# The convolution stage of a hybrid mixer: gate rows, fourth tap and norms moved among its blocks

## What is computed

```python
def causal_dwconv_silu(x, w):                 # CONV_K = 4 taps, each channel by itself
    y = lax.conv_general_dilated(x, w.astype(x.dtype)[:, None, :], ..., padding=[(CONV_K - 1, 0)], feature_group_count=x.shape[-1])
    return jax.nn.silu(y)

def hybrid_mixer(h, w_in, conv_w, a_log, dt_bias, ...):
    proj = h @ w_in
    qkv_a, z_a, b_a, a_a, qkv_b, f_b, gates = split_cols(proj, IN_SIZES)
    qkv_a = causal_dwconv_silu(pad_front(qkv_a), conv_w)          # 3072 channels
    qa, ka, va = split_cols(qkv_a, (A_QK, A_QK, A_V))
    qa = l2_norm(qa.reshape(B_, Lp, H_A, DK_A)) * (DK_A ** -0.5)  # 8 heads of 128
    ka = l2_norm(ka.reshape(B_, Lp, H_A, DK_A))
    beta = pad_front(jax.nn.sigmoid(b_a))                         # 8 columns
    g = pad_front(-jnp.exp(a_log) * jax.nn.softplus(a_a + dt_bias))
    o_a = gated_delta_rule(qa, ka, va, beta, g)[:, PAD:]
    ...
    log_f = jax.nn.log_sigmoid((f_b + f_bias).astype(jnp.float32))
    o_b = forgetting_attention(pad_front(qb), pad_front(kb), pad_front(vb), pad_front(log_f))[:, PAD:]
    ...
```

## Time and profile before

| | |
|---|---|
| median of 3 runs | 2016.93 us (2012.76 to 2021.17) |
| the profiled execution | 2013.64 us, of which 2012.3 us are the span of the profile |
| TensorE busy | 1793.0 us, 89% of the span |
| VectorE, ScalarE, GpSimd busy | 1237.6, 705.1, 434.5 us |
| mean granted clock of TensorE | 0.933 |

### The profile page before, as it was taken

One profiled execution on the slowest core, in us unless ns is written; L12 is line 12 of the kernel. 1 busy time (PEld: TensorE's weight loads), 2 busy tenths in 40 slices (PEclk: granted clock), 3 DMA queues, 4 the chain that ended last, 5 costly groups with the idle time before them and its releaser, 6 DMA issues. The chain is left out here.

```text
span 2012.3 us, 23773 instructions
## 1 busy us (share of the span) xinstructions
PE 1793.0 (89%) x9472; PEld 1356.0 (67%) x9472; DVE 1237.6 (62%) x2172; ACT 705.1 (35%) x1201; POOL 434.5 (22%) x373
## 2 busy tenths in 40 slices
PE   7989999999999989799989999977887878787878
PEld 6869988877899869678979778874333333333333
DVE  4766645765566448545464455767777667666754
ACT  4545534344455344533342343422212121212211
POOL 0330000400000000003022000014554544454541
PEclk9989999999999979889999998988998988889889
DMA  6324554444455533312221212567999999999996
GB/s 263 118 92 168 189 188 168 168 168 167 152 191 186 189 121 126 126 37 83 92 86 62 84 64 84 202 269 291 421 421 422 422 421 422 421 421 422 421 422 249
DMA packets 62621, 453.57 MB, mean 225 GB/s; under 512 B 6944, under 2 KB 7072, under 8 KB 7856
## 3 DMA queue, kind: packets, MB, share of 16 engines
q0 software_dynamic: 36864, 268.45, 32.1%
q1 hardware_dynamic: 25040, 178.27, 24.6%
q10 hardware_dynamic: 608, 5.34, 0.7%
HBM read 450.98 MB, written 1.05 MB: 225 GB/s over the span
## 5 line engine op out<-in xcount | busy, mean ns | idle before, releaser
L2330 PE MATMUL banks<-uv_rows,diag 128*128 128x512 f32 x1024 | 511.3, 663 | 125.8 <-ACT diag L2379 125.8
L548 DVE TENSOR_TENSOR weights_lo<-weights,weights_hi 128x1024 fp32r<-128x1024 f32 x336 | 419.4, 1289 | 258.6 <-ACT weights_hi L539 258.4
L2330 PEld LDWEIGHTS banks<-uv_rows,diag 128*128 128x128 f32 x1024 | 216.1, 214 | 420.4 <-issue 266.1
L539 ACT ACTIVATE weights_hi<-weights 128x1024 fp32r<-128x1024 f32 x336 | 336.7, 1051 | 391.7 <-PE banks L555 383.4
L553 PE MATMUL banks<-x_hi,weights_hi 128*128 128x256 f32 (+1 forms) x1472 | 428.0, 291 | 19.6 <-ACT key_scores L2345 12.0
L555 PE MATMUL banks<-x_hi,weights_lo 128*128 128x256 f32 (+1 forms) x1472 | 421.4, 286 | 0.0
L554 PE MATMUL banks<-x_lo,weights_hi 128*128 128x256 f32 (+1 forms) x1472 | 421.2, 286 | 0.0
L2454 DVE CUSTOM_DVE_ANT_0 uv_rows<-uv_rows,tokens 128x1024 f32<-128x1024 f32 x256 | 306.2, 1224 | 166.5 <-DMA uv_rows<-expert_uv,index 166.3
L2475 POOL DMA_INDIRECT uv_rows<-expert_uv,index x256 | 314.2, 1227 | 357.5 <-PE banks L2330 274.6
L553 PEld LDWEIGHTS banks<-x_hi,weights_hi 128*128 128x128 f32 x1472 | 283.5, 193 | 28.3 <-DVE weights_lo L548 14.8
L555 PEld LDWEIGHTS banks<-x_hi,weights_lo 128*128 128x128 f32 x1472 | 283.0, 192 | 0.0
(11 more groups left out here) (378 smaller groups left out, 2294.4 us busy)
## 6 DMA issues: line engine op xcount, KB each, us to landing
weights<-weights SPq DMA_DIRECT2D x168, 1024.0 KB, 4.7
uv_rows<-expert_uv,index POOLq DMA_INDIRECT x256, 19.2
sb_first<-constants_first ACTq DMA_DIRECT2D x1, 1920.0 KB, 8.4
sb_peer<-constants_peer ACTq DMA_DIRECT2D x1, 1544.0 KB, 6.8
sb_always<-constants_always ACTq DMA_DIRECT2D x1, 1467.0 KB, 13.8
h<-x SPq DMA_DIRECT2D x1, 1024.0 KB, 5.6
out<-h SPq DMA_DIRECT2D x4, 256.0 KB, 5.0
sb_now<-constants_now ACTq DMA_DIRECT2D x1, 216.0 KB, 4.6
```

The source lines that it names most:

```text
L539: self.act.activation(self.w_hi[b % SLOTS][:, f], self.raw[b % SLOTS][:, f], ACT.Copy).then_inc(self.hi_made, 1)
L548: self.dve.tensor_tensor(self.w_lo[b % SLOTS][:, f], self.raw[b % SLOTS][:, f], self.w_hi[b % SLOTS][:, f], ALU.subtract).then_inc(self.lo ...
L2330: mm = pe.matmul(self.bank(2 * t + half), self.diag[:, k, :], self.uv[n % NUV][:, f], start=(u < NT and k == 0), stop=(u >= UNITS - NT and ...
```

## The change

- The 24 gate columns are padded to 72, each group of 8 at a multiple of 32, and made by one product of 24 matmuls with 72 output rows, into bank 6, behind block 0; their halves small_hi and small_lo are made ahead of the mixer's pieces. Block 0 waits for x_lo piece by piece.
- The gate chain is cut into four steps, `scalar_lam(i)` and `vector_lam(i)`, behind blocks 0 to 3. Two copies from PSUM are added (to bring rows 32 and 64 to partition 0).
- The fourth tap is ScalarE's: it writes conv_out from PSUM with the weight as scale, and VectorE adds three taps. Blocks use three pairs of banks; 6 and 7 are for gates, token columns and row sums.
- Silu runs block by block, one to four blocks behind, with the squares of blocks 0 to 7; token columns stand behind block 5, the row sums behind blocks 7 and 9, the roots in ScalarE's block 10.
- Row copies and scaling go in eight rounds of two heads. Three fills (0 to 2) stand ahead of, amid and behind them; points 12, 16 and 18 of the first group of the delta rule are left out, so the fills from there on have other numbers.
- The wait for all silu moves into the first group of the delta rule.

```diff
@@ weight_stream, constants
-    small = small.reshape(KD, P, 3 * H2).transpose(1, 0, 2).reshape(P, -1)
+    small = np.pad(small.reshape(KD, P, 3, H2), ((0, 0), (0, 0), (0, 0), (0, 32 - H2)))
+    small = small.reshape(KD, P, 96)[:, :, 0:SMALL_W].transpose(1, 0, 2).reshape(P, -1)
-DELTA_POINTS = ([i for i in range(26) if i not in (2, 25)], [0, 1, 3, 4, 5, 6, 7, 8, 11, 14, 17, 20, 21, 22, 23, 24])
-FILL_AT = {(g, p): sum(len(x) for x in DELTA_POINTS[:g]) + i for g in range(2) for i, p in enumerate(DELTA_POINTS[g])}
+SMALL_W = 64 + H2
+CONV_FILLS = range(0, 3)
+DELTA_POINTS = ([i for i in range(26) if i not in (2, 12, 16, 18, 25)], [0, 1, 3, 4, 5, 6, 7, 8, 11, 14, 17, 20, 21, 22, 23, 24])
+FILL_AT = {(g, p): len(CONV_FILLS) + sum(len(x) for x in DELTA_POINTS[:g]) + i for g in range(2) for i, p in enumerate(DELTA_POINTS[g])}
@@ scalar_mixer_norm, vector_mixer_norm: first
+        self.act.activation(self.small[0][:, :, :], self.C["small"].rearrange("p (k n) -> p k n", k=KD), ACT.Copy).then_inc(self.small_hi_made, 1)
+        dve.tensor_tensor(self.small[1][:, :, :], self.C["small"].rearrange("p (k n) -> p k n", k=KD), self.small[0][:, :, :],
+                          ALU.subtract).then_inc(self.small_lo_made, 1)
@@ tensor_small
-        pe.wait_ge(self.turned_lo.sem, self.turned_lo.at("mixer", KD))
-        for g in range(3):
-            for k in range(KD):
-                mm = self.product(self.bank(4 + g, SM)[0:H2, :], [y[:, k, g * H2:(g + 1) * H2] for y in self.small],
-                                  [y[:, k, :] for y in self.x], k == 0, k == KD - 1)
+        for k in range(KD):
+            mm = self.product(self.bank(6, SM)[0:SMALL_W, :], [y[:, k, :] for y in self.small], [y[:, k, :] for y in self.x],
+                              k == 0, k == KD - 1)
@@ scalar_small, vector_small become scalar_lam(i), vector_lam(i), i = 0 to 3; new in vector_lam
+            then(dve.tensor_copy(row("y"), self.small_rows(1)))
...
+            then(dve.tensor_copy(row("y"), self.small_rows(2)))
@@ tensor_conv
+    def conv_bank(self, s):
+        return self.banks(2 * (s % 3), 2, SM)
...
-            if s >= 4:
-                pe.wait_ge(self.freed_a.sem, self.freed_a.at(name, s - 3))
+            if s >= 3:
+                pe.wait_ge(self.freed_a.sem, self.freed_a.at("conv", s - 2))
...
+                    if s == 0 and sub == 0:
+                        pe.wait_ge(self.turned_lo.sem, self.turned_lo.at("mixer", k + 1))
...
+            if s == 0:
+                self.tensor_small()
+            elif s == 5:
+                self.tensor_token_columns()
+            elif s in (7, 9):
+                j = (s - 7) // 2
+                pe.wait_ge(self.rms_sq.sem, self.rms_sq.at("conv", 4 * (j + 1)))
+                if j:
+                    pe.wait_ge(self.tok_ready, 2)
+                for k in range(H2):
+                    mm = pe.matmul(self.conv_sums(j), self.C["to_row"][:, k * H2:(k + 1) * H2], self.conv_sq[j][:, k, :], start=(k == 0),
+                                   stop=(k == H2 - 1))
+                mm.then_inc(self.rms_sums.sem, 1)
+        pe.wait_ge(self.rms_read.sem, self.rms_read.at("conv", 2))
+        self.tensor_fill(CONV_FILLS[0])
+        for c in range(8):
+            pe.wait_ge(self.rms_ready.sem, self.rms_ready.at("conv", c // 4 + 1))
+            if c < 3:
+                pe.wait_ge(self.freed_a.sem, self.freed_a.at("conv", st.n - 2 + c))
+            else:
+                pe.wait_ge(self.rms_scaled.sem, self.rms_scaled.at("conv", c - 2))
+            for j in range(2):
+                hd = 2 * (c % 4) + j
+                mm = pe.matmul(self.bank(2 * (c % 3) + j, SM), self.C["pick"][:, hd * P:(hd + 1) * P], self.row(self.ROOTED[c // 4]),
+                               start=True, stop=True)
+            mm.then_inc(self.rms_rows.sem, 1)
+            if c % 4 == 3:
+                self.tensor_fill(CONV_FILLS[1 + c // 4])
@@ scalar_conv
+        behind = {4: (0, 1), 5: (2, 3), 6: (4, 5), 7: (6,), 8: (7,), 9: (8,), 10: (9,), 11: (10,)}
...
-            act.activation(self.conv_in[:, at:at + 2, pad:], self.cols_bank("conv", s, SM), ACT.Copy).then_inc(self.freed_a.sem, 1)
-        act.wait_ge(self.cols_done_v.sem, self.cols_done_v.at("conv", st.n))
-        parts = self.conv_parts()
-        for x in parts[0:2]:
-            act.activation(x, x, ACT.Silu).then_inc(self.conv_silu, 1)
-        act.wait_ge(self.conv_silu, 2)
-        self.scalar_row_squares("conv", parts[0:2], [x[:, :, :] for x in self.conv_sq])
-        act.activation(parts[2], parts[2], ACT.Silu).then_inc(self.conv_silu, 1)
-        act.preload_act_table_set(LN_EXP)
-        self.scalar_row_roots("conv", 2, SM)
+            act.activation(self.conv_in[:, at:at + 2, pad:], self.conv_bank(s), ACT.Copy)
+            for sub in range(2):
+                j = 2 * s + sub
+                moved = act.activation(self.conv_out[:, j, :], self.conv_bank(s)[:, sub, :], ACT.Copy, scale=w[:, j, pad:pad + 1])
+            moved.then_inc(self.freed_a.sem, 1)
+            if s < 4:
+                self.scalar_lam(s)
+            for old in behind.get(s, ()):
+                self.scalar_conv_silu(old)
+            if s == 10:
+                act.preload_act_table_set(LN_EXP)
...
+        self.scalar_fill(CONV_FILLS[0])
+        self.scalar_conv_silu(st.n - 1)
+        for i in CONV_FILLS[1:]:
+            self.scalar_fill(i)
+
+    def scalar_conv_silu(self, s):
+        act, x = self.act, self.conv_out[:, 2 * s:2 * s + 2, :]
+        act.wait_ge(self.cols_done_v.sem, self.cols_done_v.at("conv", s + 1))
+        act.activation(x, x, ACT.Silu).then_inc(self.conv_silu, 1)
+        if s < 8:
+            act.wait_ge(self.conv_silu, s + 1)
+            act.activation(self.conv_sq[s // 4][:, 2 * (s % 4):2 * (s % 4) + 2, :], x, ACT.Square).then_inc(self.rms_sq.sem, 1)
@@ vector_conv
-            for tap in range(CONV_K):
+            for tap in range(pad):
...
+            if s < 4:
+                self.vector_lam(s)
+            elif s == 5:
+                self.vector_token_columns()
+            elif s in (8, 10):
+                j = (s - 8) // 2
+                dve.wait_ge(self.rms_sums.sem, self.rms_sums.at("conv", j + 1))
+                dve.tensor_scalar(self.row(self.ROOTED[j]), self.conv_sums(j), 1.0, EPS, ALU.mult, ALU.add).then_inc(self.rms_read.sem, 1)
+        for c in range(8):
+            x = self.conv_out[:, 2 * c:2 * c + 2, :]
+            dve.wait_ge(self.rms_rows.sem, self.rms_rows.at("conv", c + 1))
+            dve.scalar_tensor_tensor(x, x, 1.0 if c // 4 else DH ** -0.5, self.banks(2 * (c % 3), 2, SM), ALU.mult,
+                                     ALU.mult).then_inc(self.rms_scaled.sem, 1)
+        for i in CONV_FILLS:
+            self.vector_fill(i)
@@ tensor_delta, before its first products
+        if group == 0:
+            pe.wait_ge(self.conv_silu, self.st["conv"].n)
```

More of the change, by code:

```diff
@@ L299, in memory @@
         delta = self.top
-        self.small = [self.place("small_" + n, [P, KD, 3 * H2], F32R) for n in ("hi", "lo")]
+        self.small = [self.place("small_" + n, [P, KD, SMALL_W], F32R) for n in ("hi", "lo")]
         self.conv_in = self.place("conv_in", [P, 8, CONV_K - 1 + SM])
@@ L1417, in row, with small_rows @@
         return self.lam[:, ("beta", "G", "nbe", "tail", "eG", "ncum", "y", "t", "u", "g").index(name), :]
+    def small_rows(self, g):
+        return self.bank(6, SM)[32 * g:32 * g + H2, :]
     def tensor_small(self):
@@ L1454, in then @@
             dve.wait_ge(step.sem, step.n)
-        dve.wait_ge(self.small_hi_made, 1)
-        dve.tensor_tensor(self.small[1][:, :, :], C["small"].rearrange("p (k n) -> p k n", k=KD), self.small[0][:, :, :],
-                          ALU.subtract).then_inc(self.small_lo_made, 1)
-        a, f = (self.bank(g, SM)[0:H2, :] for g in (5, 6))
-        dve.wait_ge(self.lam_exp_b, 1)
-        then(dve.tensor_scalar(row("u"), row("u"), 1.0, None, ALU.add))
-        then(dve.reciprocal(row("beta"), row("u")))
@@ L1504, in token_scalar @@
         return self.tok[0:TILES[t][1], o:o + 1]
-    def scalar_row_squares(self, name, xs, squares):
-        for x, sq in zip(xs, squares):
-            self.act.activation(sq, x, ACT.Square).then_inc(self.rms_sq.sem, 1)
-    def tensor_row_sums(self, name, squares, width):
-        pe = self.pe
-        for j in range(len(squares)):
-            sums = self.bank(7 - j, width)[0:H2, :]
-            pe.wait_ge(self.rms_sq.sem, self.rms_sq.at(name, j + 1))
-            for k in range(H2):
-                mm = pe.matmul(sums, self.C["to_row"][:, k * H2:(k + 1) * H2], squares[j][:, k, :], start=(k == 0), stop=(k == H2 - 1))
-            mm.then_inc(self.rms_sums.sem, 1)
@@ L1536, in tensor_row_scale @@
-    def tensor_row_scale(self, name, n, width):
-        pe = self.pe
-        for j in range(n):
-            rows = self.lam[:, 9 - j, 0:width]
-            pe.wait_ge(self.rms_ready.sem, self.rms_ready.at(name, j + 1))
```

(22 more changed lines are left out.)

165 lines of the change are left out of this document (69 added, 96 removed).

## The result

| | before | after |
|---|---|---|
| median, same chip, 7 runs each | 2016.93 us (2012.73 to 2026.83) | 2004.72 us (1999.89 to 2005.57) |
| ratio, 95% interval | | 0.992 (0.9894 to 0.9945) |
| the profiled execution / its span | 2013.64 / 2012.3 us | 2005.08 / 2003.8 us |
| TensorE busy; mean granted clock | 1793.0 us; 0.933 | 1798.0 us; 0.93 |

The changed kernel is faster by 12.2 us, where 22.4 were forecast.

What follows compares the result with a forecast made beforehand. TensorE, busy 89% of the span, was taken to set the end, with time to gain only where it waits or runs at lower clock; 1.5 + 12.1 + 6.8 + 2 = 22.4 us off 2013.64 gave 1991 us, range 1979 to 2006.

Steps and rivals of the forecast that it cites:

- Term 1: From the last turned input piece to the last block's end: 86.9 us instead of 88.4, a gain of 1.5.
- I take no stall: In the blocks, VectorE and ScalarE deliver the lo halves in time: no TensorE stall (range 0 to 2.8 us).
- Term 2: Tail from the last block's end to the delta rule: 22.8 us instead of 34.9, gain 12.1 (6.0 to 15.7).
- all warm: The tail if the clock stayed at full rate throughout: 19.2 us.
- Term 3: Delta rule's levels, three half blocks fewer: 9.3 us less 0.9 and 1.6 for waits, gain 6.8 (4.5 to 8.8).
- a clock below 1 in the levels: Sign in the new profile, in the delta rule's levels, that would prove the prediction wrong.
- slower case: Clock falls in the delta rule's levels, at 0.50 throughout up to 45 us more: 2036 us; chance 0.03.
- Term 4: Delta rule's head: first rows and half block warm instead of at half clock, gain 2 us (0 to 3.5).
- Term 5: Early in the kernel: constants_always grows by 0.2 MB on a queue nothing awaits then, 0 us.
- warmer case: Clock stays up in the tail, nothing shows in the levels: 32 us gained, 1982 us; chance 0.14.
- colder one: Tail all at 0.50, splits late by 2 us in the blocks: 10.5 us gained, 2003 us; chance 0.17.
- the gates are not hidden: TensorE waits 2 us and more at each of blocks 3 to 7: 2001 to 2006 us; chance 0.04.

Runs made afterwards that it cites:

- a_wide: The changed kernel with all row copies made over 128 input rows, 120 of them zeros: 1972.86 us, 0.9768 of the kernel before.
- b_pad: The kernel before with constants_always longer by 384 unused columns, as long as in the changed kernel: 2020.91 us, ratio 1.0008.
- a_lean: The changed kernel with constants_always at its old length, the padding of the small halves made on the chip: 1996.57 us, 0.9873 of the kernel before.
- b_again: The kernel before run once more, unchanged, to see the scatter: 2021.17 us, 0.9998 of itself.
- a_fillsback: The changed kernel with half blocks back at points 12, 16 and 18 of the delta rule, none among the row copies: 2013.76 us, 0.9933 of the kernel before.
- a_batch: The changed kernel with all silu, squares, row sums and roots behind the last block again: 2012.25 us, 0.9958 of the kernel before.

## Why the prediction was right, and by how much it was off

**Term 1, up to the end of the last block.** Forecast 86.9 us; 831.7 - 746.0 = 85.7. The gate product takes 3.0 us (753.14 to 756.1), the row sums 3.83 each, and no lo half is late, so "I take no stall" held. Block 0 spends 2.9 us at 0.51, where 4.7 were assumed. ScalarE's silu and square took 0.66 us each and its tap 0.43, where 0.5 and 0.36 were taken; the slack carried it. So 1.2 better.

**Term 2, the tail.** Forecast 22.8; 24.5 measured. Step by step from the last block's end, measured against forecast: first half block done 3.6 (3.6), fourth round starts 7.9 (8.2), second half block starts 10.0 (9.3), four rounds start 15.7 (14), third half block starts 19.9 (18.3), end 24.5 (23). The misses are two of one kind. The clock, expected down "at about 9", was already down in the first rounds (0.82 over 3.6 us from 835.3), so the fourth round took 2.1 instead of 1.05. And the second half block, expected "cold at first (4.7...)", was cold to its end, 5.7. The four rounds behind it and the third half block came as forecast. In the two repeats the tail took 23.0 and 21.7, so 22.8 lies inside what one program shows. By its own steps the text's "all warm" is about 19.6 us and not 19.2; a_wide, all warm, took 18.7.

**Term 3, the levels.** Forecast 6.8; 78.6 - 71.9 = 6.7. Of the waits for dM these show behind a wait of ScalarE's copy:

```profile
930.80 0.36 PE L1797 MATMUL banks<-dMm,dTm 16*16 16x16 f32 x8 [0.20 <-ACT dMm L1871]
960.85 2.05 PE L1797 MATMUL banks<-dM,dT 128*128 128x128 f32 x16 [1.08 <-ACT dM L1871]
```

One of them is 1.08, over the bound of 1 that the text set. The sum is right, but its parts are not: of the 2.5 us set down for waits 1.28 came, and TensorE's busy time fell by 8.1 us (77.05 to 68.96) instead of 9.3, at clock 0.96 instead of 0.98. That the two misses cancel is luck. The text also named a clock below 1 in the levels as proof against it, and 0.96 is below 1. That sign was badly set: it came from 917 to 984 us, and over the whole of the levels the kernel before has 0.98. The slower case's fall, at 0.50 throughout, did not come.

**Term 4, the head.** Forecast 2; 46.3 - 43.9 = 2.4 (0.9 and 1.1 in the repeats).

**Term 5, the constants.** 0, and b_pad and a_lean say 0 within their intervals.

Together 22.0 against 22.4, with misses of 1.2 and 1.7 us in the first two terms that go against each other. **The step that failed is the one that is not in the sum:** that the rest of the kernel takes the time that it took. The whole gained 12.2, little over half of the forecast, and 2004.72 lies 1.3 us inside the upper end of the stated range, which was not drawn with these losses in mind; that it held is in part luck. The head of the second group, the same instructions, took 40.7 to 40.8 us in the three profiles of the old program (before, b_again, b_pad), and 43.6 to 46.5 in the nine of the changed program and its variants with narrow rows; the stretch before the experts took 249.0 to 251.6 in the changed program against 245.3 and 245.5. In both the row copies with 8 input rows stand, and the granted clock fell (in the head 0.85 in the changed kernel and 0.98 in b_again):

```profile
1010.00:1050.80 40.80, 34.76 (x274) 31.62 (x274) 29.20 (x50) 21.69 (x47) 7.54 (x6) 0.98 0.23 78
```

With 128 rows that head is 40.1 and 40.3 in either program, so the narrow copies are what it takes. Why the changed program met the fall there and the three profiles of the old one did not is not settled; a shift in time ahead of it was not tried by itself, and of the renumbered fills a_fillsback shows that it is not they. For the later stretch the line between the programs is not clean: b_pad has 251.5, a_batch 244.9. The early 3.6 us are not explained: one program gave 729.7 to 735.1, but eight of the ten traces of the changed side stand above all four of the other (730.1 to 732.3).

The 12.2, 15.2 and 24.3 us of the three rounds do not follow from the sum less these losses, which would be 9.0 by the first pair of profiles. The losses are differences to short executions of the kernel before, as said above, and what its longer ones lose at which stage no trace shows. With wide rows in both programs the later stretches take nearly the same time (40.1 and 40.3, 237.3 and 238.5). There the three stages differ by 21.6 us (15.5, -0.7 and 6.8) and the medians by 26.4. That supports the sum for the stages, and the clock behind them as what hides part of it; why the medians give more than the stages is open.

**The rule of the Trainium skill** (TensorE: Matmul & The Clock Gate, A second HAM failure mode: psum-queue depth-cycling) on TensorE that pauses between groups while it cycles through its banks: with three pairs of banks this trace does not agree. The blocks run at clock 0.98 over 85.7 us, 1.00 behind the first 2.9, without a stall or a fall. In the rounds the clock fell while TensorE was busy without a pause, and a_wide, with the same rounds and banks and a longer wait among them (1.43 us), kept 1.00. What decided was the input rows, not the cycling. The prediction named the narrow products as a reason "for" its slower case, and missed that they act in both heads and before the experts as well.

**The rivals.** The warmer case (1982) failed at the clock. The colder one (2003) hit the median by another way: the tail was not cold throughout, and no split was late. That the gates are not hidden was refuted by 85.66 of 85.70 us busy.

## What to carry to other kernels

Look for TensorE products with few input rows that stand in stretches of low granted clock: padding the rows with zeros cost their own time nothing here and kept the full clock in the tail and both heads. It was worth 28.4 and 17.2 us, as much as the whole restaging. Work that is spread block by block behind a busy TensorE comes out as its sum says; what such a sum cannot give is the clock of the stages behind, so list the stretches there that already sit near a fall, and keep their scatter in the range. Where fills are moved, price the clock that they hold up, not only the gap that they close.

## What the runs showed of the hardware

- Among products with 8 input rows the granted clock went from 1.00 to 0.50 while TensorE was busy for 3.60 of 3.60 us; with 128 rows, all but 8 of them zero, it stayed at 1.00 over the 18.70 us of the tail with 1.89 us idle. At full clock 8 records take 2.10 us with 8 rows and 2.00 with 128.
- The row sums have 128 input and 8 output rows. They ran at full clock among the blocks: 16 records in 3.83 us, the same as a_wide's copies with 128 by 128. So few output rows did no such harm over that time.
- Being busy is not all, with 128 rows either: from 735.1 to 746.0 us, while the pieces are turned (small products, 128x128 and 16x16), TensorE is busy for 10.90 of 10.90 us at 0.50. What of these products keeps the clock down was not tried.
- A half block behind such copies takes 3.2 us at full clock and up to 5.7 at 0.50, so a fall costs the dense work behind it as well: 2.5 us there, against some 1 us for a round of four records (2.1 instead of 1.05).
